# GpSimd instead of VectorE forms the four half combinations of the second chunk of h in turn 0

## The reference

```python
h = rmsnorm(x, mix_norm)
b_gate, c_gate, v = split(h @ conv_w_in, 3)         # 2048 x 6144
u = c_gate * v
y = causal depthwise convolution of u, width 3
x = x + (b_gate * y) @ conv_w_out                    # 2048 x 2048
a = relu(rmsnorm(x, mlp_norm) @ mlp_w1)              # 2048 x 8192
out = x + (a * a) @ mlp_w2                           # 8192 x 2048
```

## Time and profile before

| | |
|---|---|
| time, median of 3 runs | 1935.72 us (1934.09 to 1935.98) |
| profiled execution, its own time | 1933.95 us |
| its span | 1932.2 us |
| PE busy | 1892.7 us, 98% |
| DVE busy | 1708.7 us, 88% |
| ACT busy | 1024.1 us, 53% |
| POOL busy | 168.0 us, 9% |

### The profile page before, as it was taken

One profiled execution on the slowest core, in us unless ns is written; L12 is line 12 of the kernel. 1 busy time (PEld: TensorE's weight loads), 2 busy tenths in 40 slices (PEclk: granted clock), 3 DMA queues, 4 the chain that ended last, 5 costly groups with the idle time before them and its releaser, 6 DMA issues.

```text
span 1932.2 us, 22414 instructions
## 1 busy us (share of the span) xinstructions
PE 1892.7 (98%) x8512; PEld 1565.1 (81%) x8512; DVE 1708.7 (88%) x1506; ACT 1024.1 (53%) x1102; POOL 168.0 (9%) x262
## 2 busy tenths in 40 slices
PE   6999999999999899999999999999999999999999
PEld 5778888888878688888888888888888888888887
DVE  6989899898998789999889898898998889888878
ACT  6753655545557376665755657655444343333332
POOL 1100011000021210111201111010000000000000
PEclk9999999999999899999999999999999999999999
DMA  9987689878699987978879789799988978887783
GB/s 360 340 291 263 226 299 392 292 258 279 243 311 378 350 277 251 345 268 327 306 268 350 269 323 305 265 377 403 365 332 326 358 293 309 336 320 280 293 329 118
DMA packets 140603, 592.93 MB, mean 307 GB/s; under 512 B 15056, under 2 KB 19152, under 8 KB 115408
## 3 DMA queue, kind: packets, MB, share of 16 engines
q1 hardware_dynamic: 102464, 457.22, 61.3%
q0 software_dynamic: 37888, 134.23, 22.7%
q10 hardware_dynamic: 144, 0.04, 0.0%
HBM read 490.77 MB, written 100.66 MB: 306 GB/s over the span
## 4 chain that ended last, share of the span: by engine, by line
PE 91%; DVE 4%; issue 2%; ACT 2%; DMA 1%; POOL 0%; ACTq 0%; DVEq 0%
PE pair L973 89%; PE pair L993 2%; DVE ring L748 1%; DVE raw L742 1%; DMA act_kept<-act 1%; ACT ring L516 1%; DVE act L710 0%; DVE sum_l_mix L779 0%; ACT quads L468 0%; DVE sum L777 0%; DMA quads<-in_xt 0%; ACT act L501 0%; DVE sum_first_mix L788 0%; ACT u_pad L579 0%; ACT sum L542 0%
## 5 line engine op out<-in xcount | busy, mean ns | idle before, releaser
L973 PE MATMUL pair<-ring,act 128*128 128x512 f32 x8064 | 1856.1, 391 | 32.8 <-DVE ring L748 18.4
L973 PEld LDWEIGHTS pair<-ring,act 128*128 128x128 f32 x8064 | 1515.1, 189 | 351.1 <-issue 30.9
L516 ACT ACTIVATE ring<-raw 128x1024 fp32r<-128x1024 f32 x672 | 710.5, 1060 | 845.9 <-PE pair L973 556.9
L748 DVE TENSOR_TENSOR ring<-raw,ring 128x1024 fp32r<-128x1024 f32 x672 | 808.5, 1219 | 152.6 <-ACT ring L516 149.9
L742 DVE TENSOR_TENSOR raw<-raw 128x1024 f32<-128x1024 f32 x320 | 376.9, 1219 | 8.2 <-DMA raw<-in_turns 0.3
L399 POOL DMA_DIRECT2D spill<-stage x140 | 81.0, 620 | 464.3 <-ACT stage L615 361.3
L412 POOL DMA_DIRECT2D raw<-in_turns x64 | 56.9, 1036 | 702.6 <-DVE raw L742 702.6
L729 DVE TENSOR_TENSOR stage<-quads,stage 128x1024 fp32r<-128x1024 f32 x70 | 85.3, 1219 | 30.3 <-ACT stage L615 28.3
L615 ACT ACTIVATE stage<-quads 128x1024 fp32r<-128x1024 f32 x70 | 73.5, 1050 | 12.8 <-DVE quads L682 10.1
L779 DVE TENSOR_TENSOR sum<-pair,sum 128x1024 f32<-128x1024 f32 x64 | 77.8, 1216 | 0.0
L542 ACT ACTIVATE sum<-pair 128x1024 f32<-128x1024 f32 x64 | 64.7, 1011 | 0.0
(11 more groups left out here) (89 smaller groups left out, 447.2 us busy)
## 6 DMA issues: line engine op xcount, KB each, us to landing
raw<-in_turns SPq DMA_DIRECT2D x192, 1024.0 KB, 7.5
act<-spill SPq DMA_DIRECT2D x304, 512.0 KB, 6.4
act<-act_kept SPq DMA_DIRECT2D x152, 512.0 KB, 8.0
spill<-stage POOLq DMA_DIRECT2D x140, 512.0 KB, 9.6
raw<-in_turns POOLq DMA_DIRECT2D x64, 512.0 KB, 9.9
act_kept<-act POOLq DMA_DIRECT2D x36, 512.0 KB, 8.8
x_tok<-in_x SPq DMA_DIRECT2D x4, 1024.0 KB, 12.7
x<-mixed SPq DMA_DIRECT2D x8, 512.0 KB, 15.7
```

The costliest lines, as they stand in the source:

```text
L516: nc.scalar.activation(ring[g % RING][:, 0], raw[:, RAW_OF[j], 2 * (s % 2):2 * (s % 2) + 2, :], ACT.Copy).then_inc(hi_ready, 1)
L748: nc.vector.tensor_tensor(ring[g % RING][:, 1], raw[:, RAW_OF[s // 2], 2 * (s % 2):2 * (s % 2) + 2, :], ring[g % RING][:, 0].bitcast(F32), ...
L973: mm = nc.tensor.matmul(bank, stationary, moving, start=(opens and k == 0 and n == 0), stop=(closes and k == NT - 1 and n == 2))
```

## The change

The four combinations of chunk 1 leave `DIRECT_FORM`, and with them the waits of VectorE's f 0 for d = 1. A new function, `form_later(f)`, makes the same four TENSOR_TENSOR on GpSimd, with the waits that each needs, and counts them on the same semaphore. The first stands in GpSimd's queue of turn 0 between the kept copies of S4 and L22 of chunk 0, the other three behind those of L22, ahead of the kept copies of chunk 1. The first waits until both halves of chunk 1 are scaled (`x_scaled`), the second for the low half of S1 of chunk 1, the fourth for the low half of L12.

```diff
--- before.py
+++ after.py
@@ -70,8 +70,7 @@
 DIRECT_SPLIT = {(0, 0): (0, 1), (0, 2): (0, 2), (0, 3): (0, 3), (0, 4): (0, 4), (0, 5): (0, 5), (0, 6): (0, 6),
                 (0, 9): (1, 0), (0, 10): (1, 1), (0, 11): (1, 2), (0, 12): (1, 3), (0, 13): (1, 4), (1, 1): (1, 5),
                 (1, 3): (1, 6)}
-DIRECT_FORM = {(0, 1): (0, 1), (0, 2): (0, 2), (0, 3): (0, 3),
-               (0, 9): (1, 0), (0, 10): (1, 1), (0, 11): (1, 2), (0, 12): (1, 3)}
+DIRECT_FORM = {(0, 1): (0, 1), (0, 2): (0, 2), (0, 3): (0, 3)}
 for _d, _v in ((2, V_OUT), (3, V_UP)):
     DIRECT_SPLIT.update({(_v, 8): (_d, 0), (_v, 9): (_d, 1), (_v, 11): (_d, 2), (_v, 12): (_d, 3), (_v, 13): (_d, 4),
                          (_v + 1, 1): (_d, 5), (_v + 1, 3): (_d, 6)})
@@ -404,6 +403,26 @@
                     if odd == v % 2 and v // 2 - 1 in SPILL_SET:
                         put_spill(SPILL_SET[v // 2 - 1], n)
 
+            def form_later(f):
+
+                pool.wait_ge(x_scaled, 6 * NT)
+                if f == 0:
+                    pool.wait_ge(act_formed, 4)
+                    pool.wait_ge(act_lo_ready, S2 + 1)
+                    o, a, b, op = direct_s[:], later["L21"], later["L22"], ALU.subtract
+                elif f == 1:
+                    pool.wait_ge(act_lo_ready, NPROD + S1 + 1)
+                    pool.wait_ge(act_formed, 5)
+                    o, a, b, op = direct_s[:], direct_s[:], later["L11"], ALU.subtract
+                elif f == 2:
+                    pool.wait_ge(act_formed, 5)
+                    o, a, b, op = later["L21"], later["L11"], later["L21"], ALU.subtract
+                else:
+                    pool.wait_ge(act_lo_ready, NPROD + L12 + 1)
+                    pool.wait_ge(act_formed, 6)
+                    o, a, b, op = later["L12"], later["L12"], direct_s[:], ALU.add
+                nc.gpsimd.tensor_tensor(o, a, b, op).then_inc(act_formed, 1)
+
             def add_t3(v):
 
                 pool.wait_ge(t_formed, formed(v, T1))
@@ -434,7 +453,11 @@
                 if stores:
                     put_mixed(q - 1, 3)
                 if v == 0:
-                    keep_act(0, S2, L12, S3, S4, L22)
+                    keep_act(0, S2, L12, S3, S4)
+                    form_later(0)
+                    keep_act(0, L22)
+                    for f in (1, 2, 3):
+                        form_later(f)
                     keep_act(1, S2, L12, S3)
                 if v == V_OUT:
                     keep_act(2, S2, L12, S3)
@@ -686,10 +709,7 @@
                 s = direct_s[:]
                 if f == 0:
                     quads_there(dve, d, 3 * NT, 4)
-                    if d == 1:
-                        dve.wait_ge(act_formed, 4)
-                        dve.wait_ge(act_lo_ready, S2 + 1)
-                    elif d > 1:
+                    if d > 1:
                         dve.wait_ge(spilled[0], 16 * stage_uses(d - 1, 0))
                     form(s, held["L21"], held["L22"], ALU.subtract, act_formed)
                 elif f == 1:
```

## The result

The change makes the kernel slower by about 4 us: 1939.3 us in the median of 14 runs (1937.48 to 1940.99) against 1935.26 of 14 (1931.24 to 1937.64), a ratio of 1.0022 with a 95% interval of 1.0015 to 1.0029. That is just past the edge of what was called no change (0.2%), with the interval on both sides of it; the median lies 0.8 us above the predicted 1938.5, inside the range and inside the forecast's own 1936.7 to 1939.6. The profiled execution took 1938.75 us, its span is 1937.0, 4.8 longer than that of before.

A forecast was written before the change was run, and what follows sets the result against it. It took the chain L22's kept copy, 5.8 us of ScalarE, then PE as the bound. Against the profiled execution's 1933.95, + 2.3 (landing) + 0.5 (clock) gave 1936.75; the median forecast was 1938.5 us, range 1934.5 to 1944.0.

The forecast's parts named there:

- the forecast: End of turn 0: L22's kept copy 0.5 to 3.4 us later, total 1936.7 to 1939.6 us; chance 0.52.
- The path: End of turn 0: L22's copy lands, ScalarE runs six instructions from S2 (5.76 us), PE's slot 12 starts 2.3 us later.
- The combination on GpSimd: First combination in GpSimd's queue from about 44.15 us: taken at 2.3 us, called the bound above.
- The landing of L22: Second half of L22's kept copy: lands at 55.5 us instead of 53.19, 2.3 us later.
- the worst row: Longest earlier transfer time, 13.8 us, applied to L22's second half issued at 47.0: landing at 60.8, 7.6 us later.
- the second case: Slower rival: L22 waits behind SP's large transfers, landing at 60.8, total 1943.8 us; decides from 56.6; chance 0.24.
- The clock: PE's restart at slot 12: the longer stand costs 0 to 1.3 us extra at reduced clock, 0.5 taken.
- nothing behind 59.15 has room to take a microsecond up: PE after slot 12's start: a microsecond won or lost there goes through to the end nearly whole.
- VectorE's value of 0: Last third of turn 0: taking four instructions, 4.9 us in all, off VectorE gains 0 on the path.
- The late kept copies of the second chunk and T3: GpSimd's queue behind the combinations: copies first issued at about 65 instead of 55.91, T3's load after them; no cost.
- a floor of 1.3: Second combination on GpSimd, ending at 52.6 or 54.5: adds nothing, but holds ScalarE 1.3 us if L22 came early.
- Slot 9: PE in turn 0: about 0.8 us late if GpSimd and VectorE exclude one another, swallowed by the stand behind slot 11.

The follow-up runs named there:

- e2: Kernel before, all combinations on VectorE, only the kept copies of L22 held back in GpSimd's queue to about 46.1 us; ratio 1.0027 (1.0017 to 1.0038).
- e1: Changed kernel with the kept copies of L22 issued ahead of the first combination, all four combinations still on GpSimd; ratio 1.0004 (0.9995 to 1.0013) to the kernel before.
- e6: Changed kernel with a semaphore for each kept product of chunk 0, S2 waiting only for its own two transfers; ratio 1.0007 (0.9998 to 1.0015) to the kernel before.
- e5: Changed kernel with SP's two x_tok transfers moved behind that of R22; ratio 1.0007 (0.9999 to 1.0016) to the kernel before.
- e8: Kernel before with a semaphore for each kept product and, in turn 0, S3 copied out of PSUM behind slot 11; ratio 1.0000 (0.9991 to 1.0009).
- e4: Kernel before with only the first combination moved to GpSimd, ahead of L22's kept copies, the other three on VectorE; ratio 1.0027 (1.0017 to 1.0037).
- e3: Kernel before with combinations 2 to 4 moved to GpSimd, the first left on VectorE, L22's copies ahead; ratio 1.0014 (1.0005 to 1.0022).

## Why the prediction was right, and where it was not

*The path.* Right: L22's late transfers, S2, six instructions of ScalarE, the copy, PE. S2 to the copy's end took 5.75 us (5.76 predicted), and e2 shows that this alone, without a combination on GpSimd, makes the whole loss; e1 and e6 show that without it 0.8 and 1.4 us are left, neither clear of 0.

*The combination on GpSimd.* 2.3 us was taken and called a bound from above; it was 2.42 and 2.37 where nothing was in its way, so it was no bound, by a tenth of a microsecond. L22 was issued at 46.25 and 46.78 (46.5 and 47.0 predicted).

*The landing of L22.* This is the term that was mis-sized: "issued at 46.5 into an empty queue, with about 1.5 us to start" gave 55.5, and it was 59.2, near the worst row. The prediction took an empty GpSimd queue for a free way. It is SP's queue that was full: nothing of q0 moved up to 50 us. No run had shown the 1.5 us to start; it was 1.1 in e5, where SP's queue moved little from 47 us on, and 3.8 here. From the first packet to the landing the two halves took about 9 us, where 7.5 were taken. The rates of 3.1 and 4.3 us a half, read from before, were those of a copy that was queued ahead of SP's x_tok, and say nothing of one that comes behind. So the second case ("the copy lands at the worst of its rows"), which was given 0.24 and decides from 56.6, is the one that the trace shows; slot 12 was 6.0 us late and not 2.3.

*The clock.* + 0.5 was taken, about 0 measured. In the windows of the changed kernel (columns as in the earlier trace rows) the clock is at 0.50 (1.2 GHz) for 3.4 us behind the restart:

```profile
65.12:68.50 3.38, 3.38 (x8) 2.70 (x9) 3.38 (x2) 3.38 (x4) 3.38 (x4) 0.50 0.64 233
```

From the start of slot 12 to the second transposes of turn 2 it took 126.66 - 65.12 = 61.54 us, before 120.88 - 59.15 = 61.73. A stand three times as long cost no more time here. That says little of the clock, for its loss doesn't reach these transposes. The second trace of the kernel before restarts at full clock: granted clock 1.00, 13 matmuls in the first 2.94 us, where the first trace had 7 in 2.95. PE's timeline there:

```profile
58.46 16.56 PE L973 MATMUL pair<-ring,act 128*128 128x512 f32 x72 [2.22 <-ACT sum L542]
75.44 22.05 PE L973 MATMUL pair<-ring,act 128*128 128x512 f32 x96 [0.41 <-DVE ring L748]
98.76 16.58 PE L973 MATMUL pair<-ring,act 128*128 128x512 f32 x72 [1.28 <-issue]
```

And yet it took 120.20 - 58.46 = 61.74 us to the same transposes. What the clock gave, about 1.4 us, PE stood away again in turn 1 (0.41 and 1.28 us here, against 0.53 in the earlier trace rows); in the changed kernel these stands are gone. So the prediction's premise that nothing behind 59.15 has room to take a microsecond up was wrong by about 1 us: what the clock costs, and 1.1 us of what e8 won at slot 12, vanish there. The loss of 5.97 us did go through, but for 0.2.

*The sum.* 6.0 for the stand, less 0.2 to turn 2, is 5.78 by the transposes; 1.0 came back in the stretch that scatters, which leaves the 4.8 of the spans. The median went up by 4.0, and 5.78 lies just outside its interval (2.9 to 5.6), so something comes back in most executions. It may go with the four combinations: in the changed kernel, e1, e5 and e6 the times rose by 0.8 to 1.6 us less than the transposes of turn 2 moved (against the mean of the two traces of before), in e2 and e4 by 0.4 and 0.7. With intervals of over 1 us to each side that is a hint and not shown. That the time fell inside the forecast is therefore partly luck: the forecast rested on a copy 0.5 to 3.4 us later, it was 6.0 later. The second case, which the trace shows, was priced at 1943.8; the time stayed below it because the copy landed 1.6 us ahead of the worst row, the clock cost nothing, and some 1.8 us came back elsewhere. The predicted 2.8 us were closer to the time than to the cause.

*The rest.* VectorE's value of 0 was right: slots 10 and 11 ran at once, and PE only stood longer. The late kept copies of the second chunk and T3 delayed no one: the stretch of 61.54 us has no new wait. e1 and e3 show what the second combination costs once L22 is in time: S2 starts 0.8 to 1.6 us later (54.06 and 54.23 against 53.29 and 52.61 in the two traces of before); the prediction named it a floor of 1.3.

*The two engines at once.* VectorE's timeline of the changed kernel:

```profile
44.80 2.60 DVE L768 TENSOR_TENSOR ring<-raw,ring 128x1024 fp32r<-128x1024 f32 x1 [1.84 <-ACT ring L539]
...
50.72 1.21 DVE L768 TENSOR_TENSOR ring<-raw,ring 128x1024 fp32r<-128x1024 f32 x1
...
63.77 1.22 DVE L768 TENSOR_TENSOR ring<-raw,ring 128x1024 fp32r<-128x1024 f32 x1
64.91 3.40 DVE L730 TENSOR_TENSOR act<-later,act 128x1024 fp32r<-128x1024 f32 x1
```

One instruction of 1.22 us took 2.60 while GpSimd's of 43.90 ran to 46.32, and another 3.40 beside that of 63.99. GpSimd's took 3.25 and 3.24 instead of 2.4 where VectorE's of 50.72 and 63.77 was running when they began. So in each of these four places the later instruction ran only when the other had ended, as the Trainium skill, SBUF — State Buffer, section "Who interferes with whom", states for a VectorE instruction with two SBUF inputs and a GpSimd one that reads SBUF; the trace agrees. Slot 9 stood 0.81 us for it, predicted 0.8, and it was swallowed.

## What to carry to other kernels

When work is put into the queue of an engine that also issues transfers, price first the transfers that stand behind it: here an instruction of 2.4 us, which itself had to wait for ScalarE until 43.9 us, put a copy of 1 MB 7.4 us later into its queue, and it then met another queue's backlog. A transfer's time to landing can't be carried from one moment to another; ask what the other queues hold at the new moment. And one semaphore over ten transfers makes the first reader wait for the last: with one for each product the same order no longer held it, and the ratio was 1.0007 in place of 1.0022.

## What the runs showed of the hardware

A transfer issued by GpSimd while SP's queue is full can get nothing for nearly 4 us (issued at 46.25, first packet behind 50.0; q1 99.5% from 46 to 49 us) and a third of the engines after, 12.4 us for 512 KB; with x_tok off SP's queue it had 8.6. The other way round, SP's transfers issued from 42.15 on had nothing up to 45.5 us behind GpSimd's. A TENSOR_TENSOR of 128 x 1024 float32 takes GpSimd 2.4 us, and beside a VectorE one of 1.22 us the two run one after the other (3.25 us on GpSimd, 2.60 and 3.40 on VectorE). One kernel restarts PE at a granted clock of 0.50 behind a stand of 2.68 us in one execution and at 1.00 behind 2.22 us in another. Taking 4.9 us of work from VectorE lowered its busy time by only 1.2 us: the two held instructions alone are 1.4 and 2.2 us longer than their 1.22.
